# Feature-major inputs for memory, x, columns and narrow weights, and later places for three groups of work, in a two-model fp32 block

## What is computed

```python
u = _rmsnorm(h, norm_w)
proj = jnp.matmul(u, w_in)                      # 2048 x 20528, split into q, k, v, gates, ...
h_a = _mlstm_chunkwise(q, k, v, i_pre, logf)    # gates from 16 + 32 narrow columns of proj
h_b = _gated_delta_chunkwise(dq, dk, dv, beta, g)
y = sigmoid(gate_a) * (h_a @ w_out[:2048]) + sigmoid(gate_b) * (h_b @ w_out[2048:])
x = _rmsnorm(h + y, final_norm_w)
for l in range(2):
    mkv = mem @ w_mem_kv[l]                     # memory keys and values
    h = x @ w_in_2[l]                           # 16 narrow columns: a low-rank gate
    y = concat(band_attention, gla, memory_attention)
    x = layer_norm(ALPHA * x + (y * silu(z)) @ w_out_2[l])
```

## Time and profile before

| | us |
|---|---|
| median of 3 runs (lowest to highest) | 2195.75 (2192.3 to 2201.71) |
| profiled execution, whole | 2195.95 |
| its span, first to last instruction | 2194.3 |
| PE busy | 2162.1 (99% of the span) |
| DVE busy | 1284.6 (59%) |
| ACT busy | 1106.3 (50%) |
| POOL busy | 134.3 (6%) |
| memory projections, first stream matmul to gate block | 10.20 to 64.20 |
| gate block | 64.20 to 68.34 |

### The profile page before, as it was taken

One profiled execution on the slowest core, in us unless ns is written; L12 is line 12 of the kernel. 1 busy time (PEld: TensorE's weight loads), 2 busy tenths in 40 slices (PEclk: granted clock), 3 DMA queues, 4 the chain that ended last, 5 costly groups with the idle time before them and its releaser, 6 DMA issues.

```text
span 2194.3 us, 32949 instructions
## 1 busy us (share of the span) xinstructions
PE 2162.1 (99%) x12515; PEld 1780.3 (81%) x12515; DVE 1284.6 (59%) x1518; ACT 1106.3 (50%) x1489; POOL 134.3 (6%) x216
## 2 busy tenths in 40 slices
PE   8999999999999999999999999999999999999997
PEld 7788888888888787787878888888888788888886
DVE  5446456454554857575765564566545845566467
ACT  6445445454444748374655454455544544445452
POOL 6000000000000000001010000000000210000001
PEclk9999999999999999999999999999999999999998
DMA  7765655656565545354546756745467476555554
GB/s 264 247 194 174 191 182 169 208 183 202 182 205 179 156 143 163 117 179 129 173 129 199 242 171 198 202 150 166 155 201 262 152 238 172 164 161 169 187 174 134
DMA packets 215620, 398.56 MB, mean 182 GB/s; under 512 B 21750, under 2 KB 38337, under 8 KB 215102
## 3 DMA queue, kind: packets, MB, share of 16 engines
q1 hardware_dynamic: 206512, 367.70, 53.0%
q0 software_dynamic: 6672, 20.63, 3.5%
q10 hardware_dynamic: 2304, 8.39, 1.1%
HBM read 387.85 MB, written 8.82 MB: 181 GB/s over the span
## 4 chain that ended last, share of the span: by engine, by line
PE 86%; ACT 5%; DVE 4%; issue 3%; DMA 1%; DVEq 0%; POOL 0%; ACTq 0%; SPq 0%
PE stream_psum L618 26%; PE stream_psum L620 25%; PE stream_psum L619 25%; PE heads_psum L599 2%; ACT work L1084 2%; ACT w_high L1084 2%; DVE w_low L1514 1%; PE heads_psum L809 1%; DVE work L1696 1%; PE heads_psum L996 1%; PE heads_psum L958 1%; PE heads_psum L939 1%; DMA w_raw<-in_w_in 1%; ACT L1084 1%; PE heads_psum L757 0%
## 5 line engine op out<-in xcount | busy, mean ns | idle before, releaser
L1514 DVE TENSOR_TENSOR w_low<-w_raw,w_high 128x1024 fp32r<-128x1024 f32 x688 | 832.6, 1228 | 627.0 <-ACT w_high L1084 624.9
L1084 ACT ACTIVATE w_high<-w_raw 128x1024 fp32r<-128x1024 f32 (+1 forms) x700 | 715.4, 1046 | 462.4 <-PE stream_psum L620 380.1
L618 PE MATMUL stream_psum<-w_high,x_high 128*128 128x512 f32 x1856 | 742.7, 400 | 2.8 <-DVE w_low L1514 2.5
L620 PE MATMUL stream_psum<-w_high,x_low 128*128 128x512 f32 x1856 | 724.5, 390 | 0.0
L619 PE MATMUL stream_psum<-w_low,x_high 128*128 128x512 f32 x1856 | 723.9, 390 | 0.0
L618 PEld LDWEIGHTS stream_psum<-w_high,x_high 128*128 128x128 f32 x1856 | 349.1, 188 | 76.9 <-DVE w_low L1514 3.9
L620 PEld LDWEIGHTS stream_psum<-w_high,x_low 128*128 128x128 f32 x1856 | 348.7, 188 | 74.1
L619 PEld LDWEIGHTS stream_psum<-w_low,x_high 128*128 128x128 f32 x1856 | 349.3, 188 | 69.6 <-issue 1.9
L618 PE MATMUL stream_psum<-w_high,y_high 128*128 128x512 f32 x896 | 355.2, 396 | 2.1 <-DVE w_low L1514 1.5
L620 PE MATMUL stream_psum<-w_high,y_low 128*128 128x512 f32 x896 | 350.1, 391 | 0.0
L619 PE MATMUL stream_psum<-w_low,y_high 128*128 128x512 f32 x896 | 349.9, 390 | 0.0
(11 more groups left out here) (310 smaller groups left out, 1197.2 us busy)
## 6 DMA issues: line engine op xcount, KB each, us to landing
w_raw<-in_w_in SPq DMA_DIRECT2D x528, 512.0 KB, 4.4
w_raw<-in_w_out SPq DMA_DIRECT2D x128, 512.0 KB, 5.2
w_raw<-in_w_mem_kv SPq DMA_DIRECT2D x32, 512.0 KB, 5.4
work<-rows_scratch POOLq DMA_DIRECT2D x8, 512.0 KB, 5.3
proj<-in_mem SPq DMA_DIRECT2D x4, 512.0 KB, 8.0
residual<-in_x SPq DMA_DIRECT2D x2, 1024.0 KB, 7.3
mkv_scratch<-proj POOLq DMA_DIRECT2D x4, 512.0 KB, 5.6
mem_high_scratch<-y_high POOLq DMA_DIRECT2D x4, 512.0 KB, 4.1
```

Of the source, the lines that this page charges most:

```text
L618: pe.matmul(acc, hi[:, k, sl(m)], w, start=first, stop=False)
L620: return pe.matmul(acc, lo[:, k, sl(m)], w, start=False, stop=final)
L1084: return act.activation(dst, src, func, **kw)
L1514: tt(WL[:, c % RING, :], RAW[:, c % RING, :], WH[:, c % RING, :].bitcast(F32), ALU.subtract).then_inc(lo_done, 1)
```

## The change

The host lays five inputs out anew before the launch: x and the memory transposed (features by tokens), all short vectors and the gate biases as one matrix of 128 rows by 275 columns, the 48 gate columns and the 16 low-rank columns of each layer as packed blocks. In the kernel:

- `mem_part` loads the memory in eight pieces of 256 KB straight into feature order; ACT and DVE split it from SBUF. The transposes of the memory, of the short vectors and of x are gone from PE, and so are the 10 small DMAs on POOL's queue.
- x is loaded twice: transposed (four times 512 KB, after chunks 8 to 11) for the features, and in rows (after chunks 12 and 14) for the norm and the residual. The features are no longer scaled by the inverse norm of the token; ACT applies it as the scale of every copy out of PSUM (`scaled=True`), DVE on the gates.
- The narrow weights have a buffer and semaphores of their own (`narrow_w`, `narrow_in`, `narrow_high`, `narrow_low`) and take no slot of the ring. The gate columns come as one DMA after chunk 13, the low-rank columns as one DMA ahead of each layer's memory chunks, behind a wait of SP for `out_lo`.
- PE runs 12 matmuls of the identity by itself (`WARM`) ahead of the first chunk.
- In `dn`, `products("qk")` stands one half chunk later on PE; DVE's `decayed` stands one step later, which moves no instruction on DVE.
- POOL's gamma products at the end wait for the low part of the last chunk.

Core of the diff:

```diff
+            def mem_part(c):
+                sp.dma_start(MEMT[:, 2 * c:2 * c + 2, :], bass.AP(mem_t.tensor, c * (2 * P * S), [[2 * S, P], [S, 2], [1, S]])).then_inc(mem_in[c], 16)
+            def x_features(i):
+                sp.dma_start(wk(i, U).rearrange("p (c n) -> p c n", c=2), bass.AP(x_t.tensor, i * (4 * P * S), [[2 * S, P], [2 * P * S, 2], [1, 2 * S]])
+                             ).then_inc(xt_in[i], 16)
             for half in range(2):
                 for c in range(NCH):
+                    if half == 0 and c >= RING:
+                        mem_part(c)
                     put(N_MEM, half * NCH + c, rows_in_chunk(w_mkv, half * NBLK, 1024, c, [[1, NBLK]]))
+                    if half == 0 and c < RING:
+                        mem_part(c)
+                    if half == 1 and c == 5:
+                        sp.dma_start(GATE_RAW, gate_cols.rearrange("p c j n -> p (c j) n")).then_inc(narrow_in, 16)
+                    if half == 1 and c < 4:
+                        x_features(c)
-            narrow(N_GATE, w_in, 0, IN1, [(C_IF, 16), (C_BA, 32)])
...
-        X_AFTER = ((0, 5), (1, 0))
+        X_AFTER = ((1, 4), (1, 6))
...
+                wait_alone(sp, out_lo, NCH + 16 * l + 32)
+                sp.dma_start(LOW_RAW, low_rank_cols[l].rearrange("p c j n -> p (c j) n")).then_inc(narrow_in, 16)
                 for c in range(NCH):
                     put(n + L_MEM, c, rows_in_chunk(w_mkv, D * 1024 + l * NBLK, 1024, c, [[1, NBLK]]))
-                narrow(n + L_LR, w_in2, off, IN2, [(C_LR, 16)])
...
             pool.wait_ge(lw_in, LW_IN[2])
+            pool.wait_ge(lo_done, N_L + 2 * LSZ)
...
+            for i in range(WARM):
+                pe.matmul(H[:, 3, 0:P], ident[:], ident[:], start=True, stop=True)
-            stream(N_MEM, E_MEM, 2, YH, YL, itertools.chain(mem_features(mem_tiles), x_prep()), features=m_lo, base=0)
+            stream(N_MEM, E_MEM, 2, YH, YL, none(), features=m_lo, base=0)
...
+                        kw = {"scale": ST[:, 4 + m:5 + m]} if scaled else {}
-                            f(PR[:, m, sl(slots[b], NBLK)], acc, ACT.Copy).then_inc(evac, 1)
+                            f(PR[:, m, sl(slots[b], NBLK)], acc, ACT.Copy, **kw).then_inc(evac, 1)
...
                 yield from gap(2)
-                yield
+                yield from gap(2)
                 pe.wait_ge(*done(DN_V, "v1", g))
                 products("qk", 2, 0)
-                yield from gap(3)
+                yield from gap(2)
```

More of the change, by code:

```diff
@@ L1084, in f, with high, narrow_high, stream @@
                 return act.activation(dst, src, func, **kw)
-            def high(n, c, extra, width=CH * NBLK):
-                act.wait_ge(loaded[c % RING], load_count(n, c, extra))
+            def high(n, c):
+                act.wait_ge(loaded[c % RING], load_count(n, c))
                 if not (isinstance(n, int) and n + c < RING):
                     act.wait_ge(used, n + (c - RING + 1))
-                if width == CH * NBLK:
-                    f(WH[:, c % RING, :], RAW[:, c % RING, :], ACT.Copy).then_inc(hi_done, 1)
-                else:
-                    f(paired(c % RING, width)[:, :, 0, :], four(RAW, c % RING, width), ACT.Copy).then_inc(hi_done, 1)
-            def stream(n, nblk, extra, side, slots=(0, 1, 2, 3), free=(), ahead=(CH * NBLK, 0), per=NCH, lead=AHEAD, following=AHEAD, base=1, values=None):
+                f(WH[:, c % RING, :], RAW[:, c % RING, :], ACT.Copy).then_inc(hi_done, 1)
+            def narrow_high(turn, w, raw):
+                act.wait_ge(narrow_in, 16 * turn + 16)
+                f(w[:, :, 0, :], raw, ACT.Copy).then_inc(narrow_hi, 1)
+            def stream(n, nblk, side, slots=(0, 1, 2, 3), free=(), ahead=True, per=NCH, lead=AHEAD, following=AHEAD, base=1, values=None, scaled=False):
                 for b in range(nblk):
@@ L1138, in x_prep @@
                 f(ST[:, 4:6], ST[:, 2:4], ACT.Exp, scale=-0.5).then_inc(norm_s, 1)
-                yield from gap(2)
-                act.wait_ge(norm_s, 4)
-                act.wait_ge(cols_v, 5)
-                for h in range(2):
-                    last = f(wk(h, U), RES[:, 0, sl(h, U)], ACT.Copy, scale=ST[:, 4:5])
-                    yield
-                last.then_inc(x_scaled, 1)
-                yield from gap(2)
-                for c in range(NCH):
-                    act.wait_ge(x_pe, c + 1)
-                    for j in range(2):
-                        k = 2 * c + j
-                        f(XH[:, k, :], H[:, c % 4, sl(j, S)], ACT.Copy, scale=NC_[:, k:k + 1]).then_inc(x_hi, 1)
-                    yield
             def gates():
@@ L1496, in _ @@
                        free=[[done(AT_PE["a"], "q", 2 * l)], [done(AT_PE["a"], "k", 2 * l)], [done(AT_PE["a"], "pv", 2 * l)], [done(AT_V["a"], "g", 2 * l)]], base=l)
                 last_heads = attend("a", q + 3, 2 * l + 1, 2 * (e + 14), 3, 4)
[L1498 to L1499 removed]
+                stream(n + L_Y1, 4, itertools.chain(last_heads, end_high()) if l else along(last_heads, load_mem(1, 5)), slots=None, per=len(Y1_TILES))
@@ L1501, in _ @@
+                stream(n + L_Y2, 4, none(), slots=None, per=len(Y2_TILES), ahead=not l, following=AHEAD if l else LEAD)
             ln_stats(1)
@@ L1961, in _ @@
             mem_feature(0)
+            low(N_MEM, 1)
             mem_feature(1)
-            low(N_MEM, 1)
-            stream(N_MEM, 2, itertools.chain(mem_features(), x_prep()), ahead=W_GATE)
-            small_block(N_GATE, 48)
+            stream(N_MEM, 2, itertools.chain(mem_features(), x_prep()))
             stream(N_ML, 4, gates())
@@ L2036, in _ @@
                 n, q = N_L + l * LSZ, 8 + 4 * l
[L2037 to L2038 removed]
+                stream(n + L_MEM, 1, ln_features() if l else rms_features(), lead=LEAD)
                 stream(n + L_M, 2, none())
@@ L2067, in _ @@
                 stream(n + L_Y1, 4, itertools.chain(last_heads, end_low()) if l else last_heads, take=take1, per=len(Y1_TILES), base=l)
-                stream(n + L_Y2, 4, none(), take=take2, per=len(Y2_TILES), ahead=None if l else CH * NBLK, following=AHEAD if l else LEAD,
+                stream(n + L_Y2, 4, none(), take=take2, per=len(Y2_TILES), ahead=not l, following=AHEAD if l else LEAD,
                        rows=(row_used, 1) if l else None, base=l)
@@ L2106 @@
     arrays, args = {}, []
-    for name in INPUTS:
-        a = np.ascontiguousarray(inputs[name])
+    for name, a in laid_out(inputs).items():
+        a = np.ascontiguousarray(a)
         arrays[f"in_{name}"] = a
```

294 lines of the change are left out of this document (117 added, 177 removed).

## The result

The changed kernel takes 2184.72 us (median of 7 runs, 2182.78 to 2186.14) beside 2194.74 (7 runs of the kernel before on the same chips). The medians are 10.0 us apart; the ratio is 0.9949, 95% interval 0.9937 to 0.9961, or 0.5% faster. Forecast were 2177 and a gain of 18.5 us, so the time lies inside the range (2171 to 2187), near its upper end, and some seven to eight microseconds are missing.

A forecast was written before the change was run, and what follows sets the result against it. PE, busy 2162.1 of 2194.3 us, was taken as the bound. Gains of 9.0 + 3.8 + 3.4 + 0.7 + 1.6 = 18.5 us off 2195.75 gave 2177.2, said as 2177, with a range of 2171 to 2187.

The forecast's parts named there:

- The start: Before the mLSTM: transposes leave PE and the first stream matmul comes earlier; mLSTM at 59.3 for 68.34, 9.0 us gained.
- The allowance of 0.5 us for waits: At the start: ACT's in-order work on x's rows or the gates' chain may hold the stream; 0.5 us taken.
- The sum of bytes: Start loads: 17.3 MB, the last 12.9 at 330 GB/s; 17th chunk there at 54.2, split at 56.5, just hidden.
- rival E: Start: 180 GB/s is the load mix's limit; mLSTM at 102, total 2220 us; chance 0.06 with its milder form.
- B: Start: late data, the mixed queue bringing 291 GB/s and not 330; cost about 6 us, total 2183; chance 0.18.
- Rival D: Start: identity matmuls bring PE to the 2.4 GHz level before the stream; 2.3 us less, total 2175; chance 0.07.
- The gap in the first mLSTM block: First mLSTM block: PE's gap (2.15 us) and the slow matmuls behind it (1.69) both go; 3.8 us gained.
- The delta-net groups: Four delta-net groups: moving the query-key products later removes the wait for `v1`, 0.86 us each; 3.4 us gained.
- Rival C: Delta-net groups: the gap only moves, to the inverse or another wait on DVE; total 2180.5 us; chance 0.09.
- the scaled copies: Copies out of PSUM with a scale: ACT perhaps 0.1 us longer each, 80 times, half idle; booked as 0.
- The low-rank blocks: Last layer's low-rank block: the gap goes with narrow weights loaded and split far ahead; 0.7 us gained.
- The end: Ahead of the final block: PE's gap goes with POOL's products behind the last low part; 1.6 us gained.

The follow-up runs named there:

- its other trace: Kernel before with only the query-key products moved one half chunk later on PE; median 2188.33 us beside 2193.99, ratio 0.9969.
- 26 products: Changed kernel plus 26 identity products of 32x32 (104 PE instructions) behind the warm-up products; one execution, 2177.38 us.
- rows later: Changed kernel with the second half of x's rows loaded after memory chunk 15 and not ahead of it; one run, 2184.2 us.
- short warm-up products: Changed kernel with 12 warm-up products of 32x32 for 128x128, and POOL's end products not waiting for the last low part; one run, 2186.15 us.
- 16 and 32 products: Changed kernel plus 16 or 32 identity products of 32x32 behind the warm-up products; single executions, 2180.97 and 2178.85 us.
- unscaled copies: Changed kernel with copies out of PSUM left without the token's inverse norm as scale, so not the same computation; one run, 2186.41 us.
- the repeat: The changed kernel run and traced once more, nothing altered; one run, 2182.84 us.
- v and key block later: Changed kernel with the transposes of v and the first key block one half chunk later on PE in each delta-net group; one run, 2185.56 us.

## Why the prediction was right and where it was not

**The start, 9.0 forecast, 8.7 measured.** The first stream matmul came at 8.66 for 8.45, the mLSTM at 59.69 for 59.3. That this is so near is in part luck: over the 12 traces with this start the mLSTM begins between 58.61 and 62.29. The allowance of 0.5 us for waits was short of the 1.7 us gap at 51; the slow matmuls at the start, 9 instead of 12, made up for part of it. The sum of bytes found the right limit, a near tie of loads and PE (56.5 against 58.8 us), and the DMA shares of 0.93, 1.04 and 0.97 show one. It was drawn up for the wrong chunk: the 17th landed at 51.93 (54.2 forecast) and held nothing up. The one that PE waited for was the 16th, at 50.43, behind x's second rows in the same queue; only the allowance stood for it. The rate of 330 GB/s that it assumed was met (311, 406, 334), so rival E fell, and of B there is only the mildest form, that one gap. Rival D, the clock, came true in most executions and brought nothing that shows, because of that near tie; its price of 2.3 us was wrong for this reason.

**The gap in the first mLSTM block, 3.8 forecast, 4.3 measured** (12.94 up to copy 4, less 8.65 at the mLSTM's start). The gap and the slow matmuls behind it went together. But of the 3.8, 1.7 are no fixed part of the kernel before: in its other trace the same gap had no slow matmuls behind it, and measured against that one the gain of the stretch is 3.3. The prediction's argument was right in kind (slow matmuls came only behind a gap), but the gap alone does not bring them: 2.38 us had them and 2.40 had none.

**The delta-net groups, 3.4 gain forecast, 3.7 loss measured.** The step itself was right: the wait for `v1` is gone, and in the kernel before the move alone gives 3.8. Rival C said that the loss would come back as a wait for DVE at the inverse; its size was near, its cause was not. Three terms make the measured +3.7:
- the wait for `v1`: -3.8, from the move alone;
- the scaled copies: +1.5. The prediction had booked them as 0.1 us each "at an engine half idle: 0". The duration was right (0.09) and the zero wrong. ACT's copies head the chain to DVE's convolution, for which PE already waited 1.2 and 0.7 us, in rows of before that the prediction does not show or use;
- PE's code, as what is left over: 3.7 + 3.8 - 1.5 = 6.0, of which 4.9 show as idle at issue in the inverse (7.0 + 0.5 + 0.4 for 3.0). The prediction has no term for it. The waits of before did list 3.0 us of idle at L809 without a releaser, and the prediction kept them unsaid, as a constant of the kernel. It was the sign of a cost that an edit of PE's code ahead of it can change: by +6.0 here, and by -2.9 with 26 products (476.22 less 1.5 for the scaled copies, for 477.60).

**The low-rank blocks, 0.7 forecast, 1.2 measured.** The gap of the earlier trace rows has no successor in the changed kernel; SP's wait for `out_lo` cost PE nothing, as taken. The rest is two small gains (copies 82 to 90, 0.4; 90 to 138, 0.8, which holds the 0.7), inside the 1.5 us over which this stretch varies among the versions.

**The end, 1.6 forecast, 1.7 measured**, and undone alone it returns to the hundredth. Of the 3.45 us, 2.34 are the two low parts' own.

So 18.5 - 7.1 = 11.4, and the other terms add 0.5 (mLSTM), 0.5 (low-rank blocks) and 0.1 (end), less 0.3 (start): the 12.2 us of the spans. The missing term of code, 6.0, made most of the 7.1, the scaled copies 1.5, and the move itself gave 0.4 back. The forecast was right in its range because the four other terms held and the range was wide enough for a loss of this size; no part of it foresaw the loss.

## What to carry to other kernels

Before pricing an edit that adds or removes instructions on the bounding engine, look in the list of waits for idle time at issue inside runs of short instructions, and for packets on the instruction queue beside it: such a place can gain or lose microseconds with the number of instructions ahead of it, and cheap ones (26 products, 104 instructions, here) at a time when the engine waits anyway can move it to a good place. Try several counts, for no row foretells the best one. An instruction that gets 0.1 us longer on a half idle engine is free only if nothing behind it on the way to the bound already waits; a wait there, however short, says that it isn't.

## What the runs showed of the hardware

- PE's code comes in packets of 16 KB, 255.6 recorded instructions apart on average. All 92 idle times without a releaser in the groups end at multiples of 256 instructions (to one), 1.19 to 1.61 us after a packet's end (770.69 to 772.00, 759.76 to 761.14; in the kernel before 898.97 to 900.43). 64 matmuls of 32x32 with their weight loads run through half a packet in 0.75 us.
- The same program has its code gaps in the same groups in every execution, to 0.6 us in two executions of one kernel (1.1 with the two of other edits at the same count, rows later and short warm-up products), and up to 4.2 us apart with 64 instructions more ahead (41.87 and 37.69, 16 and 32 products), 5.3 with 128 more.
- After 4.5 to 5.5 us of 128-column products the first chunk ran at 2.4 GHz in some executions and at 1.2 GHz for 7 to 9 matmuls in others; the changed kernel's two traces are one of each. After gaps of 2.26, 2.37 and 2.44 us between starts, at 51 to 54 us in three of the runs (unscaled copies, 32 and 26 products), seven or eight matmuls ran at 0.43 us. Gaps of 2.34 (the repeat), 2.40 (the query-key move alone) and 2.52 (v and key block later) had none behind them. The length of a gap of this size does not decide it here.
- VectorE's subtraction of 1024 columns takes 1.21 to 1.23 us by itself. Of the two beside GpSimd's products in SBUF the first took 1.22 and the second 2.30 (3.45 for both, against 2.34), and GpSimd's two products took 1.30 and 2.20, for 1.29 each alone.
- ScalarE's copy of 512 columns out of PSUM takes 0.60 us, and 0.68 with a scale for each partition.
